# Expert weights in runs of 8 KB, with the channels dealt to the partitions to match

## The reference, cut to what matters

```python
def hier_moe(x2d, w_group, b_group, w_expert, b_expert, w1, w3, w2):
    ...                       # combine[t, e]: the weights of the 2 experts of token t, of 16
    def expert_step(acc, p):
        w1e, w3e, w2e, c = p  # (1024, 512), (1024, 512), (512, 1024)
        h = jax.nn.silu(x2d @ w1e) * (x2d @ w3e)
        return acc + c[:, None] * (h @ w2e), None
...
h = layernorm(ALPHA * h + f, post_ln_g[l, 1], post_ln_b[l, 1])   # f: the mixture's output
```

## Time and profile before

| | us |
|---|---|
| median of 3 runs (lowest, highest) | 854.68 (852.52, 858.32) |
| profiled execution, first to last instruction | 855.4 |
| PE busy in it, VectorE, ScalarE | 717.0, 310.5, 218.0 |
| HBM read, written | 181.84 MB, 11.01 MB |

### The profile page before, as it was taken

The page is one execution under the profiler, slowest core; times in us unless marked ns, Lnnn a source line. Parts: engine busy times, 40 slices in busy tenths (PEclk is TensorE's granted clock), DMA queues, the critical chain, the costliest instruction groups (busy, mean ns, idle before and its releaser), DMA issues.

```text
span 855.4 us, 17692 instructions
## 1 busy us (share of the span) xinstructions
PE 717.0 (84%) x6878; PEld 458.2 (54%) x6879; DVE 310.5 (36%) x932; ACT 218.0 (25%) x528; POOL 20.2 (2%) x38
## 2 busy tenths in 40 slices
PE   5999989979989989755559999969974799998864
PEld 4887858545555645422228647747841455554431
DVE  0599951362212222200063305871153122221215
ACT  1213660331212212200340013564050022222220
POOL 0000000000000000000110001100000000000001
PEclk9999989989999999977668999999997799999986
DMA  9998043305885989999589947040436995947924
GB/s 302 347 348 307 1 136 126 120 0 199 303 308 193 341 292 330 310 310 330 182 299 343 362 174 256 39 147 1 150 128 217 350 328 194 328 154 260 305 72 148
DMA packets 94858, 193.30 MB, mean 226 GB/s; under 512 B 8144, under 2 KB 22329, under 8 KB 94825
## 3 DMA queue, kind: packets, MB, share of 16 engines
q1 hardware_dynamic: 80880, 176.24, 58.5%
q10 hardware_dynamic: 11673, 8.10, 3.2%
q0 software_dynamic: 2272, 8.52, 2.7%
HBM read 181.84 MB, written 11.01 MB: 225 GB/s over the span
## 4 chain that ended last, share of the span: by engine, by line
PE 48%; DMA 26%; DVE 18%; issue 4%; ACT 3%; SPq 1%; POOL 0%; DVEq 0%; ACTq 0%; POOLq 0%
DMA ring<-in_moe_w 22%; PE ps L636 12%; DVE work L1093 9%; PE ps L657 6%; PE ps L563 4%; PE ps L535 3%; PE ps L546 3%; PE ps L716 3%; PE ps L735 3%; PE ps L474 2%; PE ps L608 2%; PE ps L508 2%; DMA work<-ybuf,pos_i 1%; DMA ring<-in_conv_w_pw 1%; PE ps L619 1%
## 5 line engine op out<-in xcount | busy, mean ns | idle before, releaser
L636 PE MATMUL ps<-ring,work 128*32 128x256 f32 x2816 | 179.3, 410 | 54.9 <-issue 30.1
L636 PEld LDWEIGHTS ps<-ring,work 128*32 128x32 f32 x2816 | 103.7, 118 | 123.1 <-issue 79.1
L1288 DVE TENSOR_TENSOR work<-work,ps 64x256 f32<-64x256 f32 x44 | 18.7, 425 | 253.5 <-ACT work L911 253.5
L825 ACT ACTIVATE work<-ps 128x256 f32<-128x256 f32 (+3 forms) x154 | 52.3, 354 | 226.0 <-PE ps L657 97.9
L657 PE MATMUL ps<-ring,work 128*32 128x256 f32 x1408 | 90.7, 386 | 1.9 <-DMA ring<-in_moe_w 1.9
L1093 DVE SCALAR_TENSOR_TENSOR work<-work,wdw 128x272 f32<-128x272 f32 x180 | 74.9, 494 | 0.0
L608 PE MATMUL ps<-tok,work 128*32 128x256 f32 x928 | 64.5, 385 | 0.0
L474 PE MATMUL ps<-xT,ring 128*128 128x272 f32 x256 | 62.3, 407 | 2.3 <-DMA ring<-in_conv_w_pw 1.8
L911 ACT ACTIVATE work<-ps 64x256 f32<-64x256 f32 x44 | 16.6, 376 | 163.3 <-PE ps L636 163.3
L657 PEld LDWEIGHTS ps<-ring,work 128*32 128x32 f32 x1408 | 39.0, 109 | 35.3 <-DVE work L1290 10.3
L474 PEld LDWEIGHTS ps<-xT,ring 128*128 128x128 f32 x256 | 50.4, 198 | 13.6 <-issue 1.9
(11 more groups left out here) (215 smaller groups left out, 726.3 us busy)
## 6 DMA issues: line engine op xcount, KB each, us to landing
ring<-in_moe_w SPq DMA_DIRECT2D x138, 1024.0 KB, 6.6
ring<-in_conv_w_pw SPq DMA_DIRECT2D x12, 1024.0 KB, 11.1
ybuf<-work ACTq DMA_DIRECT2D x44, 128.0 KB
ybuf<-const POOLq DMA_DIRECT2D x2, 2048.0 KB, 7.9
ring<-in_kv_w_k SPq DMA_DIRECT2D x4, 1024.0 KB, 6.6
ring<-in_kv_w_v SPq DMA_DIRECT2D x4, 1024.0 KB, 6.5
ring<-in_attn_w_q SPq DMA_DIRECT2D x4, 1024.0 KB, 6.1
ring<-in_attn_w_o SPq DMA_DIRECT2D x4, 1024.0 KB, 5.4
```

The lines of the kernel that those rows point to most:

```text
L636: last = pe.matmul(ps[SLOTS * q:SLOTS * (q + 1), 0, 0:256], xTg[:, k, :], w[:, k, (q % 2) * 256:(q % 2 + 1) * 256], start=(k == 0), stop=( ...
L825: return act.activation(dst, src, ACT.Copy)
```

## The change

Each half of a brick is read in runs of 8 KB for each partition. For w1 and w3 partition p holds rows 8p to 8p+7 as chunks 0 to 7, and a half is four consecutive rows. For w2 the half a (256 rows) gives partition p rows 256a + 2p and 256a + 2p + 1. The number of loads, their bytes, order and waits stay.

The channels must follow. In `tok`, channel 8x + k now stands in column 128k + x, so that the gather and its transposes, unchanged, bring channel 8p + k to partition p of chunk k. ACT's copy writes `tok` with a step of 128 elements (512 bytes) from one channel to the next. What reads `tok` in the order of the channels reads with that step: the identity matmul L519 and the addition L1309, which is now made in pieces of 512 channels. The transposes of h (L644) take every second column of h.

```diff
+        def tok_columns(rows, j, half):
+            return tok[0:rows, j, :].rearrange("t (k x) -> t x k", k=NC_)[:, 64 * half:64 * half + 64, :]
+        def by_eight(t):
+            return t.rearrange("t (x k) -> t x k", k=NC_)
...                                  # SP, expert()
-                    load_half(b + m, half, NC_ if m < 2 else 4, src.rearrange("(k p) n -> p k n", p=P))
+                    if m < 2:
+                        load_half(b + m, half, NC_, src.rearrange("(p k) n -> p k n", p=P))
+                    else:
+                        sp.dma_start(brick(b + m).rearrange("p (a m n) -> p a m n", a=2, m=2)[:, half],
+                                     src.rearrange("(a p m) n -> p a m n", a=2, m=2)[:, half]).then_inc(sem(f"brick{(b + m) % RING}_{half}"), 16)
...                                  # PE, combine()
-                    pe.matmul(ps[:, 6 + j, :], ident, tok[:, j, half], start=True, stop=False)
+                    pe.matmul(ps[:, 6 + j, :], ident, tok_columns(P, j, 1), start=True, stop=False)
...                                  # PE, item()
-                    last = pe.transpose(ps[:, 4, m * 64:(m + 1) * 64], hs[64:128, m * P:(m + 1) * P], ident[64:128, 64:128])
+                    last = pe.transpose(ps[:, 4, m * 64:(m + 1) * 64], hs[64:128, m:256:2], ident[64:128, 64:128])
...                                  # ACT, post()
-                        move(tok[0:rows_, j, half * 512:(half + 1) * 512], ps[0:rows_, 2 * j + half, :]).then_inc(sem(f"tok_ready{l}"), 1)
+                        move(tok_columns(rows_, j, half), by_eight(ps[0:rows_, 2 * j + half, :])).then_inc(sem(f"tok_ready{l}"), 1)
...                                  # DVE, combine()
-                    step(dve.scalar_tensor_tensor(first, first, wts[0:n, 0, j:j + 1], tok[0:n, j, 0:w], ALU.mult, ALU.add))
+                    for h in range(w // 512):
+                        part = by_eight(first[:, h * 512:(h + 1) * 512])
+                        step(dve.scalar_tensor_tensor(part, part, wts[0:n, 0, j:j + 1], tok_columns(n, j, h), ALU.mult, ALU.add))
```

## The result

The changed kernel is slower, where a small gain was forecast: 860.62 us (median of 11 runs, 850.22 to 862.65) against 852.52 (11 runs, 848.94 to 858.32) for the kernel before, a ratio of 1.0073 with a 95% interval of 1.0039 to 1.0106. That is +6.2 us (3.3 to 9.0). It is within the 1% called "same", but its sign is clear, and 860.6 lies inside the range of the prediction, near its upper end.

A forecast was written before the change was run, and what follows sets the result against it. It took expert-weight loads and PE's matmuls to bound the kernel in different stretches. Loads -3.6, split addition +0.2 and stepped tok reads +0.6 gave -2.8 us; less 0.7 to the median, 851.9 us, range 840 to 862.

The forecast's parts named there:

- the 182 us that the chain named: Stretches of both layers where the chain runs through half bricks alone; only these 182.2 us could gain from a better load.
- two signs of being wrong: Steps of the load chain shorten by more than 4%, or the chain leaves the loads and the time moves anyway.
- The load term, -3.6 us: Weight loads in the 182 us: longer runs gain 2%, -3.6 us, between ends of -11.3 and +10.6 us.
- the two queues' line: Packet cost fitted through queues q1 and q0: 10.8 ns a packet plus 40.5 ns per 1000 B, making packets 6.9% cheaper.
- The first rival (844.2 us): Weight loads: the packet's price is paid in full, -11.3 us plus 0.8 for tok; chance 0.33.
- The second rival (866.1 us): Weight loads: longer runs load more slowly, +10.6 us plus 0.8 for tok; chance 0.08.
- The transposes of h: Weight loads of L644 where PE decides, 137 ns each: taken at 0, upper end +6.8 us if the load doubled.
- VectorE's step: Additions on the path reading tok with the step, 2.83 us: a fifth more, +0.6 us; upper end +5.7.
- ScalarE's copies and the identity matmul: Copies to tok and L519: cost 0, covered by 4.25 us and 1.8 us of slack.
- The rival of a dear step: At tok, the step of 512 bytes triples durations: 863.4 us; chance 0.07.
- The fetches: PE's instruction fetches at the start of layer 1's mixture: taken at 0, between -4 and +5.2 us.
- Runs merged: q1's packets fall from 80880 by 41,216; the rival that runs stay short, 855.5 us, had chance 0.08.

The follow-up runs named there:

- experiment 4: The kernel before with three halves in flight instead of two: 837.52 us, ratio 0.9830 to the kernel before.
- 9: The changed kernel with three halves in flight and four store buffers instead of two: 834.57 us, ratio 0.9807 to the kernel before.
- 13: The kernel before with three halves in flight and four store buffers: 836.29 us, ratio 0.9850 to the kernel before.
- experiment 2: The changed kernel with its packets cut to 2 KB (w1, w3) and 4 KB (w2), order kept: 862.42 us, ratio 1.0129 to the kernel before.
- experiment 3: The changed kernel with w2 loaded as before (4 KB runs) and h transposed without a step: 853.11 us, ratio 1.0020 to the kernel before.
- experiment 11: The kernel before with only w2 in 8 KB runs and the transposes of h with a step of two: 854.51 us, ratio 1.0037.
- 12: The kernel before with w2's new order and stepped transposes, but w2's packets cut to 4 KB: 853.10 us, ratio 1.0037.
- 14: The changed kernel with the step moved from the transposes to ScalarE's and VectorE's reads of PSUM: 852.83 us, ratio 1.0005 to the kernel before.
- 1: The changed kernel run again with no edit: 858.68 us, ratio 1.0076 to the kernel before.
- 8: The changed kernel with packets cut to 2 KB and 4 KB and three halves in flight: 839.45 us, ratio 0.9872 to the kernel before.
- 5: The changed kernel with three halves in flight, two store buffers: 847.99 us, ratio 0.9964 to the kernel before.
- 15: The changed kernel with three halves in flight, four store buffers and the step moved to reads of PSUM: 829.94 us, ratio 0.9767 to the kernel before.

## Why the prediction was wrong

**What bounds the kernel: right in place, wrong in cause.** The time that depends on the load is the 182 us that the chain named. But "only these 182 us can gain from a better load" was priced as if the packets set its pace wherever the engines are 0.90 busy. With two halves in flight the depth holds the pace back: a third half gives 14 us with the same packets (experiment 4), and with the engines full the stretches show the price of a packet clearly (115.6 us in 9 against 125.2 in 13). Neither of its two signs of being wrong came as written: the steps did not shorten by 4%, and the chain did not leave the loads. What could be traced of the loss lies outside the 182 us, in the items and the additions.

**The load term, -3.6 us.** Its size can't be settled at two halves in flight: the profiled stretch of layer 0 went from 138.1 to 140.5 and 142.7 us, while experiments 2, 3, 11, 12 and 14 had 139.9, 135.5, 139.3, 137.6 and 137.0, long packets or short. Experiment 2 allows a gain of 0 to 9 us; 12 against 11, on w2 alone, gives 0 +- 3.5. The mean price of 8 KB fell by 1.3% only (375 to 370 ns), against 6.9% by the two queues' line. That line mixed the tail of q1 with packets of another queue. That its 6.9% lie near the 6.4% of the medians is luck. Where the engines were full, the mean price fell by 10% (9 against 13). The first rival (844.2 us) needed the price to fall with two in flight and did not get it. The second rival (866.1 us) was drawn from w2's longer steps; experiment 2 speaks against it, since the kernel with short packets is not faster, and 12 shows no effect of w2's length.

**The transposes of h, taken at 0: the step that failed.** "As if paced by their 128 columns" was read out of rows that all had unit step, which can't show what a step does. They took 203 ns for 137, half of the upper end's doubling, and the pair stands on the chain of every item that PE decides. The items grew by 0.11 us in layer 0 and 0.07 in layer 1, which is 1.8 us on the two chains; the price in the whole time is 3.1 us (experiment 11, 0.6 to 5.7) to 6 us (14 against 1, +- 4.5). This is most of what the change lost: with the step moved away the kernel is level with the one before (1.0005), though the gain that was forecast is not seen there either.

**VectorE's step, taken at a fifth, was half.** With the split, 1.3 to 1.65 us on the path for the 0.8 of the forecast. The whole of experiment 3's loss is of that size.

**ScalarE's copies and the identity matmul: right.** The copies took 1.8 times as long, below the 2.4 times that the cover allowed: in layer 0 they end at 178.48 us, and the warm-up begins at 180.66. The matmul kept its 2.05 us, so its cover was never tried. The rival of a dear step had the place partly right and the factor of three wrong: 1.8 for the copies, 1.5 for the additions, 1 for the matmul.

**The fetches: right**, unchanged. **Runs merged: right**, to the packet.

The sum by what was found, 0 for the load (not settled), 1.8 for the transposes and 1.65 for VectorE, is 3.4 us against a measured 6.2 (3.3 to 9.0). The rest, 2.8 us, stays open. It is not above the noise, and experiments 11 and 14 put the transposes higher than the chains do; but experiment 2, with all of the order and none of the length, lies 11 us (7 to 15) above the kernel before, and 3.4 us do not explain that. With three halves in flight the same comparison (8 against 4) gives 3.6 us +- 5.5.

## What to carry to other kernels

A DMA share of 0.9 does not say that packets set the pace: put one more transfer in flight first, and judge longer runs only when the share is 1. Longer packets on one queue delayed the short transfers of another here, so look at those transfers' buffers in the same edit. Rows that all have unit step say nothing on what a step costs: such a term needs a price in the sum, not a 0. Where data must be permuted, put the step where it was seen to be free, in ScalarE's and VectorE's reads of PSUM or in PE's moving operand, and not in a weight load or in a VectorE operand in SBUF. What an operation costs more counts only where its engine decides.

## What the runs showed of the hardware

**A step costs by engine and side.** Float32 with a step of 512 bytes in SBUF: VectorE with one of its two tensor inputs so read 1.05 us for 0.70 (512 channels), ScalarE's write 0.90 for 0.50, PE's moving operand 2.05 for 2.05. These patterns also have inner rows of 8 elements where there was one of 512, and no run separates the step from that. With a step of 8 bytes PE's weight load 203 ns for 137; reads of PSUM by ScalarE and VectorE nothing. The Trainium skill (Advanced Engine Details and Errata, Memory Cachelines) asks for two hits on a line of 16 bytes, which a step of 8 bytes still has: for the weight load the trace does not agree. With 512 bytes no line is hit twice in a row; VectorE and ScalarE pay, as the page has it, and PE's moving operand does not. For PSUM the same section wants every two elements contiguous for matmuls; ScalarE's and VectorE's reads with a step of 8 bytes showed no price, and no run here has a matmul writing so.

**Short stores behind long packets.** With two weights' halves in flight a store of 128 KB in 1 KB packets landed after 5.4 us behind 2 KB and 4 KB packets and after 7.6 us behind 8 KB ones (5.8 with the packets cut); with the engines full 8.0 and, behind 8 KB, 11 to 14, up to 35 us when four stores were allowed at once. The Trainium skill (DMA: Bandwidth & Descriptors, Queues, rings and completion order) says that an engine takes its queues in turn and switches only between packets, a packet there being a bundle of descriptors, which a record of the trace need not be; the trace agrees in direction, and no run here shows how long a turn is.

**The tail of long packets.** A quarter of the 8 KB packets' time was spent in packets over one and a half times the median at two halves in flight, a tenth with three (9 to 11 parts in 100 in experiments 5, 9 and 15). Of the 4 KB packets' time it is a fifth in the kernel before and 11 parts in 100 in experiment 13, of the 2 KB packets' 13 and 15. What makes the tail was not found.
